# Sample rows added on TensorE and copied by ScalarE, an earlier mark of the prompts' choices, and one expert step ahead of the slot table

## The reference

```python
y  = y + concat(attention, other) @ w_out          # residual, per token
xf = rmsnorm(y, norm_ffn)
g_logits = xf @ router_g + router_g_b              # 4 groups
e_logits = xf @ router_e + router_e_b              # 16 experts
g_idx = argmax(g_logits)                           # one group per token
top_v, top_i = top_k(e_logits in that group, 2)    # two experts per token
y  = y + sum over the two experts of gate * down(silu(gate_e(xf)) * up_e(xf))
```

## Time and profile before

| what | us |
|---|---|
| median of 3 runs | 594.43 |
| the profiled execution | 593.07 |
| its span in the profile | 591.1 |
| TensorE busy in it | 570.3 |
| VectorE, ScalarE, GpSimd busy | 247.6, 154.0, 85.8 |

### The profile page before, as it was taken

How to read it: one execution, slowest core, us unless ns; L and a number is a source line. 1 busy time by engine, 2 the same in 40 slices (tenths; PEclk the granted TensorE clock), 3 DMA queues, 4 the chain that set the end, 5 groups by cost and what they waited for, 6 DMA issues and landing times. The chain is left out here.

```text
span 591.1 us, 8584 instructions
## 1 busy us (share of the span) xinstructions
PE 570.3 (96%) x3462; PEld 322.9 (55%) x3462; DVE 247.6 (42%) x597; ACT 154.0 (26%) x329; POOL 85.8 (15%) x113
## 2 busy tenths in 40 slices
PE   6999999999989999999999999999999999999993
PEld 5677877545733333336977555667655653333331
DVE  6999674213733221145551705251113652221147
ACT  6142185221300101124234203244103310101123
POOL 5991700000012120000100001000000021120000
PEclk9899999999999999999999999999999999999998
DMA  8994899996699999999799998999789999999972
GB/s 333 409 343 63 195 410 368 403 422 277 238 398 406 420 421 420 396 324 414 314 422 330 400 412 299 324 337 409 314 348 416 363 394 411 424 419 419 388 244 92
DMA packets 39930, 208.94 MB, mean 354 GB/s; under 512 B 12819, under 2 KB 14547, under 8 KB 23920
## 3 DMA queue, kind: packets, MB, share of 16 engines
q1 hardware_dynamic: 30416, 169.92, 73.4%
q0 software_dynamic: 7872, 34.53, 16.2%
q10 hardware_dynamic: 1600, 3.90, 1.7%
HBM read 198.76 MB, written 43.74 MB: 410 GB/s over the span
## 5 line engine op out<-in xcount | busy, mean ns | idle before, releaser
L1486 PE MATMUL bank<-arena 128*64 128x512 f32 x264 | 85.4, 598 | 0.0
L1486 PE MATMUL bank<-ring,arena 128*64 128x512 f32 x232 | 74.4, 598 | 0.5 <-DVE arena L1814 0.5
L2273 PE MATMUL bank<-arena,ring 128*128 128x320 f32 x256 | 71.6, 434 | 0.0
L2273 PEld LDWEIGHTS bank<-arena,ring 128*128 128x128 f32 x256 | 48.0, 190 | 21.3 <-issue 1.6
L1410 PE MATMUL bank<-ring,arena 128*128 128x512 f32 x104 | 45.4, 594 | 1.0 <-PEq L451 0.6
L572 PE MATMUL bank<-xnT,ring 128*128 128x320 f32 x144 | 41.2, 447 | 0.5 <-DVE xnT L890 0.5
L1486 PEld LDWEIGHTS bank<-arena 128*64 128x64 f32 x264 | 24.2, 136 | 31.3 <-issue 31.0
L1517 PE MATMUL bank<-arena 128*64 128x512 f32 x136 | 39.8, 594 | 0.7 <-ACT arena L1724 0.7
L1931 DVE COPY arena<-bank 128x512 f32<-128x512 f32 x14 | 9.7, 691 | 68.3 <-PE bank L1517 68.3
L1517 PE MATMUL bank<-ring,arena 128*64 128x512 f32 x120 | 36.1, 593 | 0.7 <-ACT arena L1724 0.7
L1486 PEld LDWEIGHTS bank<-ring,arena 128*64 128x64 f32 x232 | 21.2, 136 | 24.9 <-issue 24.7
(11 more groups left out here) (447 smaller groups left out, 873.0 us busy)
## 6 DMA issues: line engine op xcount, KB each, us to landing
arena<-in_w_moe SPq DMA_DIRECT2D x50, 1024.0 KB, 16.0
ring<-in_w_moe SPq DMA_DIRECT2D x44, 1024.0 KB, 14.3
arena<-in_stream_b SPq DMA_DIRECT2D x4, 2560.0 KB, 14.9
out_o_d_old<-in_cache_d_g POOLq DMA_DIRECT2D x1, 8448.0 KB, 29.9
arena<-in_stream_a SPq DMA_DIRECT2D x4, 2048.0 KB, 11.2
out_o_d_old<-in_cache_d_g POOLq DMA_DIRECT2D x1, 7680.0 KB, 43.6
out_o_d_old<-in_cache_d_g SPq DMA_DIRECT2D x1, 4608.0 KB, 37.8
ring<-in_w_out_even SPq DMA_DIRECT2D x2, 2048.0 KB, 11.9
```

The source lines that it names most:

```text
L1486: last = nc.tensor.matmul(c.bank[2 + j % 2][half, :], xgT[:, j % 2, q, half], w[i][q // 4][:, q % 4, :], start=(q == 0), stop=(q == KC - 1))
L2273: last = nc.tensor.matmul(bank(name)[:, 0:TOK], w[:, k, i * P:(i + 1) * P], xnT[:, k, :], start=(k == 0), stop=(k == KC - 1))
```

## The change

Four edits, in both layers:

1. Samples: TensorE first multiplies the residual rows by the identity into bank 4 and then accumulates `w_out`'s product on top, so PSUM holds the sum. ScalarE copies it to `resid` in two halves and counts up `s_added`; VectorE's `add(2)` is gone.
2. VectorE: `mark(0, 2)` follows `choose(0, 2)` directly, and `place(0, 2)` stands ahead of `mean(2)`.
3. TensorE: the four `keep_clock_up` matmuls ahead of the samples' turn become one, and the one behind `places` is gone.
4. The first step of the first pair's `up` stands ahead of the slot table's product, and VectorE does `first_turned(0)` ahead of `L`.

Beside these, a list of semaphores has two entries instead of three, as many as are used.

```diff
@@ TensorE, samples @@
 def project_samples(first, end):
+    if first == 0:
+        for h in range(2):
+            nc.tensor.matmul(c.bank[4][64 * h:64 * h + 64, :], c.ident[0:64, 0:64],
+                             c.resid[0:64, 2, h * 512:(h + 1) * 512], start=True, stop=False)
     for q in range(first, end):
         for h in range(2):
             last = nc.tensor.matmul(c.bank[4][64 * h:64 * h + 64, :], parts[q][:, SEQ:TOK],
-                                    where[q][:, h * 512:(h + 1) * 512], start=(q == 0), stop=(q == n_parts - 1))
+                                    where[q][:, h * 512:(h + 1) * 512], start=False, stop=(q == n_parts - 1))
@@ TensorE, the list @@
 project_samples(n_parts - 3, n_parts)
-c.keep_clock_up(c.bank[7], 4, 256)
+c.keep_clock_up(c.bank[7], 1, 256)
+pe.wait_ge(s_added, 2)
 turn_rows(2)
 pe.wait_ge(tri_ok, 1)
 pe.wait_ge(sel_ok, 1)
 places((0, 1)).then_inc(pos_pe, 1)
-c.keep_clock_up(c.bank[0], 1, 192)
 logits(2)
...
 gather_first(2)
+up(0, 0, 1)
 pe.wait_ge(H_ok, 1)
 pe.wait_ge(S_ok, 1)
...
-up(0, 0, KC)
+up(0, 1, KC)
@@ ScalarE @@
 for t, rows in enumerate(ROWS):
-    act.wait_ge(added, 2 * t + 2)
+    if t < 2:
+        act.wait_ge(added, 2 * t + 2)
+    else:
+        act.wait_ge(done, 6)
+        for h in range(2):
+            nc.scalar.copy(c.resid[0:rows, 2, h * 512:(h + 1) * 512],
+                           c.bank[4][64 * h:64 * h + 64, :]).then_inc(s_added, 1)
+        act.wait_ge(s_added, 2)
@@ VectorE @@
 choose(0, 2)
-add(2)
 mark(0, 2)
 apply_gain(2)
+place(0, 2)
 mean(2)
-place(0, 2)
 choose(2, 3)
...
+first_turned(0)
 v.tensor_tensor(m["L"], ...).then_inc(S_ok, 1)
-first_turned(0)
 first_turned(1)
```

More of the change, by code:

```diff
@@ L115, in __init__ @@
         self.ring_dn = [nc.alloc_semaphore(f"ring_dn{i}") for i in range(SLOTS)]
-        self.xg_in = [nc.alloc_semaphore(f"xg_in{i}") for i in range(3)]
+        self.xg_in = [nc.alloc_semaphore(f"xg_in{i}") for i in range(XG)]
         self.y_out = [nc.alloc_semaphore(f"y_out{i}") for i in range(2)]
@@ L1179, in moe_block @@
     sel_ok, pos_pe, S0_ok, tmp_ok, idx_pe, idx_ok = s("sel"), s("pe_pos"), s("onehot0"), s("place"), s("pe_idx"), s("idx")
-    lg_read = s("logits_read")
+    lg_read, s_added = s("logits_read"), s("samples_added")
     diag_ok, summed, cnt_ok, g_in, rows_final = s("diag"), s("summed"), s("overflow_count"), s("final_gain"), s("final_out")
@@ L1414, in project_samples @@
             def project_samples(first, end):
+                if first == 0:
+                    for h in range(2):
+                        nc.tensor.matmul(c.bank[4][64 * h:64 * h + 64, :], c.ident[0:64, 0:64], c.resid[0:64, 2, h * 512:(h + 1) * 512],
+                                         start=True, stop=False)
                 for q in range(first, end):
@@ L1418, in project_samples, with turn_rows @@
                         last = nc.tensor.matmul(c.bank[4][64 * h:64 * h + 64, :], parts[q][:, SEQ:TOK],
-                                                where[q][:, h * 512:(h + 1) * 512], start=(q == 0), stop=(q == n_parts - 1))
+                                                where[q][:, h * 512:(h + 1) * 512], start=False, stop=(q == n_parts - 1))
                 if end == n_parts:
                     last.then_inc(done, 2)
-            def turn_rows(t):
+            def turn_rows(t, halves=(0, 1)):
                 rows = ROWS[t]
-                pe.wait_ge(added, 2 * t + 2)
-                for h in range(2):
+                if t < 2:
+                    pe.wait_ge(added, 2 * t + 2)
+                for h in halves:
+                    if t == 2:
+                        pe.wait_ge(s_added, h + 1)
                     for q in range(4):
@@ L1704, in _ @@
             for t, rows in enumerate(ROWS):
-                act.wait_ge(added, 2 * t + 2)
+                if t < 2:
+                    act.wait_ge(added, 2 * t + 2)
+                else:
+                    act.wait_ge(done, 6)
+                    for h in range(2):
+                        nc.scalar.copy(c.resid[0:rows, 2, h * 512:(h + 1) * 512], c.bank[4][64 * h:64 * h + 64, :]).then_inc(s_added, 1)
+                    act.wait_ge(s_added, 2)
                 nc.scalar.activation(xn[0:rows, t], c.resid[0:rows, t], ACT.Square,
@@ L1782, in add @@
                     r = c.resid[0:ROWS[t], t, h * 512:(h + 1) * 512]
-                    ps = c.bank[2 * t + h][0:ROWS[t], :] if t < 2 else c.bank[4][64 * h:64 * h + 64, :]
-                    v.tensor_tensor(r, ps, r, ALU.add).then_inc(added, 1)
+                    v.tensor_tensor(r, c.bank[2 * t + h][:, :], r, ALU.add).then_inc(added, 1)
             def mean(t):
```

## The result

The changed kernel took 598.36 us in the median of 20 runs (594.86 to 606.63), the kernel before 594.41 in the median of 20 (591.45 to 597.17). The ratio is 1.0066, with a 95% interval of 1.0046 to 1.0086: slower by 3.9 us. Both kernels scatter by more than their difference, so that one profile shows one draw. The profiled execution of the changed kernel took 599.21 us.

What follows compares the result with a forecast made beforehand. TensorE, busy 570.3 of 591.1 us, was taken to bound the kernel. 0.05 + 0.05 (both routings) + 2.3 (second gather) = +2.4 us, making the median 596.8; range 594.1 to 599.0.

Steps and rivals of the forecast that it cites:

- a late second gather: Second routing: the gather for the second pair's rows starts 0.7 us late, lands 1.6 slower; TensorE's turn 2.3 us late.
- its own signs: Second routing's profile: granted clock 1.00, gather landing in 5.5 to 8 us; landing in 4.8 makes the forecast wrong.
- a term that stood in the sum as 0: Removing idle matmuls ahead of the samples' turn and logits was counted as costing 0 us.
- The samples' path: Samples' products to their turn: identity products 0.9 us, two copies 1.07 together; the turn begins 0.05 us later per routing.
- its bound: ScalarE's two copies ahead of the samples' turn run one by one, 2 x 0.59 us, making the turn +0.15.
- What is removed was cover, not path: 0.: Ahead of the samples' turn, the removed idle matmuls only filled time when TensorE waited for the add: 0 us.
- Rival C: Clock falls after TensorE's idling around the turns, or loads go first in full: 599 to 605 us, chance 0.10.
- the loads' full price: Second gather waits for the weight loads in full: 0.7 + 3.2 = 3.9 us.
- Place ahead of mean: Second routing: place's move gains nothing, the mean comes 0.6 us later, x_rows is issued about 0.6 us late.
- Up ahead: First up step ahead of the slot table's product: TensorE's sum unchanged, 0; slot table about 0.9 us later, before x_rows lands.
- The gather: Second routing: starts at 478.75, loads at 479.38; lands in 6.4 us, bounds 4.8 and 8.0; turn 2.3 us late.
- the line that the prediction drew through two rows: Gather 1.33 us ahead of the loads landed in 4.8 us, one just behind in 9.3; 3.2 over 1.4 us blamed on loads.

Runs made afterwards that it cites:

- e2: Kernel before with one unread matmul instead of four ahead of the samples' turn and none behind places: 595.47 us, ratio 1.0024.
- e6: Kernel before with all five unread matmuls removed: 598.52 us, ratio 1.0099.
- e3: Kernel before with place(0, 2) moved ahead of mean(2), nothing else: 597.19 us, ratio 1.0030.
- e4: Kernel before with the first up step ahead of the slot table's product and first_turned(0) ahead of L: 593.79 us, ratio 0.9998.
- e5: Changed kernel with unread matmuls fitted to the waits, two of 256 columns and one of 192: 595.87 us, ratio 1.0042.
- e1: Changed kernel with all five unread matmuls back, four of 256 columns and one of 192: 596.76 us, ratio 1.0043.
- e11: The changed kernel run again, unaltered, for a second profile: 596.27 us, ratio 1.0057.
- e12: Changed kernel with fitted unread matmuls (two of 256 columns, one of 192), the same version as e5 run again: 595.36 us, ratio 1.0027.
- e8: Changed kernel with mean ahead of place again, up behind the slot table again, and fitted unread matmuls: 594.72 us, ratio 1.0027.
- e7: Kernel before with two unread matmuls of 256 columns added ahead of a softmax wait in the first mixer: 595.05 us, ratio 1.0036.
- e9: Changed kernel with fitted unread matmuls, second-layer loads of the fourth up step held until the first gather landed: 598.60 us, ratio 1.0086.
- e10: Kernel before with second-layer loads of the fourth up step held until the first gather landed: 596.64 us, ratio 1.0049.

## Why the prediction was right, and where it was wrong

It said 596.8 us, 2.4 more than before, with a range to 599.0. Measured: 3.9 more, 598.36. Direction and size held. Of its mechanism only a part did: of the 2.4 us, 2.3 were to be a late second gather. By its own signs (a gather that lands in 4.8 us, a granted clock other than 1.00) the forecast was wrong in both profiles of the changed kernel: the gather landed in 4.5 and 4.3 us and the clock fell. What was paid there was a term that stood in the sum as 0. That the time still fell into the range is in part luck.

*The samples' path.* Predicted +0.05 us per routing. From the samples' first product to the turn it is now 460.32 to 470.03, 9.71 us, against 9.40 before (from 457.35, where line 1418 begins in its timeline, to 466.75): +0.3. Two terms of the sum were each 0.1 too small: the identity products take 1.0 us and not 0.9, and the copies (580 ns each) do not overlap, 1.18 us and not the 1.07 of the earlier trace rows; the prediction had this last one as its bound.

*"What is removed was cover, not path: 0."* This step failed. The matmuls took no time on the path, but their cover was the clock. e2 and e6 show its price with nothing else changed: 0.24% for four of the five, hardly clear of none, and 1.0% for all. Both profiles of the changed kernel show the fall in the second routing. Rival C had this with a chance of 0.10, together with the loads' full price; against it the prediction set a stretch that idled 1.04 us in 8 without a fall. Such a stretch shows that a fall need not come, not that it will not.

The Trainium skill, "TensorE: Matmul & The Clock Gate", section "Why this matters for your kernels", warns against gaps between bursts of matmuls, but names only longer ones than those that the removed matmuls had filled. By that row alone their removal would have been no risk, other than the prediction read it. The measurement decides: gaps of 0.66 and 0.43 us stood ahead of both falls in the changed kernel.

*Place ahead of mean.* `x_rows` 0.6 us later: measured 0.55 (470.03 to 473.54, against 2.96). Right. Its landing was taken as 0.7 late; in the profile of e3 the gather was not late at all (11.31 us behind the turn, 11.30 before).

*Up ahead.* Predicted 0, measured +0.2 per layer (e4's profile), within the noise of its times. The slot table was to come 0.9 us later and before `x_rows` landed: its product came 1.1 us later in e4 (the sum had taken 2/3 of the first gather for its third quarter), and in the profile of the changed kernel, where the clock's fall came on top, the gather waited for the table.

*The gather.* Predicted: issued 0.63 us ahead of the loads, 6.4 us to landing, 2.3 us lost, as one fixed number. The profiles of the second routing, by the time between gather and loads: 0.26 us, 9.1 to landing (e2); 0.86, 6.8 (e5); 1.0, 4.7 (e1); 1.2, 4.3 (e11); 1.3, 4.7 to 5.1 (before, e3, e12); 1.4, 5.7 (e8); 1.5 to 1.8, 4.5 to 5.1 (e4, e6, changed, e7). The direction of the line that the prediction drew through two rows is borne out, on two late gathers, one of them in an execution that was the longest of its kernel. Its slope is not: 3.2 us over 1.4 would give 7.2 and 5.9 us for these two. And e8's 5.7 us, like e9's 5.4 with the loads held back, shows that the time to landing also moves without the loads.

What the prediction took for fixed is a draw: with no fall of the clock at the place, the gather began 10.8 us behind the samples' turn in e7 and 12.4 in e2, in both of which `x_rows` was issued 2.96 us behind it. In both profiles of the changed kernel the fallen clock delayed the fourth up step and so these loads, and the gather got away: the two losses may exclude one another, as far as two profiles tell.

The Trainium skill's rule of round-robin between queue rows ("DMA: Bandwidth & Descriptors", section "Queues, rings and completion order") would let the gather's 512 KB go at half the rate. With 1.3 us for them at the full rate, as in the prediction, that is an estimate of 1.3 us more than the 4.8. The 6.8 and 9.1 us are more than that.

What the pieces are worth together, as far as the runs tell them apart: instructions, 0.5 us per routing (0.3 at the turn, 0.2 at up), 1.0; beside them the clock's fall (3.2 and 1.6 us in the two profiles of the changed kernel) or TensorE's wait for the gather (0.4, 2.6 and 0.4 in e1, e5 and e12). Restoring the matmuls in full or fitted gives 1.0043, 1.0042 and 1.0027, against 1.0066 and 1.0057 as changed: the intervals overlap, so the times alone don't show the clock's share. The granted clock of every execution, which is on record beside its time, says more:

| executions | number | mean clock |
|---|---|---|
| kernel before, beside e1 to e12 | 111 | 0.9922 |
| changed kernel (the 20 of the result, e11) | 32 | 0.9872 |
| changed, matmuls back or fitted (e1, e5, e12) | 36 | 0.9917 |
| e2, four of five removed | 13 | 0.9896 |
| e6, all removed | 10 | 0.9827 |
| e3, no matmul touched | 12 | 0.9894 |

An estimate: a mean clock lower by 0.001 costs 0.6 us of the 595, as TensorE is nearly always busy. So e6's 0.0100 against its own rounds (0.9927) is 5.9 us, about its whole loss. e3 lies 0.003 low without a matmul touched, so that a difference of this size, e2's for one, proves little alone. The changed kernel lies 0.0045 below its versions with the matmuls back (95% interval 0.0023 to 0.0066, over different chips), an estimated 2.7 us; its mean time is only 1.3 us longer, 597.90 against 596.58. With the matmuls back the clock is that of the kernel before, and the mean time is still 2.7 us longer than its 593.89. 1.0 of these are the instructions above (2.2 in e1, with its 0.6 per layer); the rest is the wait for the gather and what the runs don't tell apart. Nothing tried beats the kernel before; e4 equals it.

## What to carry to other kernels

An unread matmul that ends before a wait does costs nothing and may be what keeps the clock; take its length from the wait, and judge its removal by many executions, by their times and their granted clocks, not by the chain of one. When a step is moved by half a microsecond, look at what is issued just behind it on another queue: a gather that had 1.3 us on a pair of 1 MB loads landed in 4.8 us, one with 0.3 us in 9.1. And hold one profile against the scatter of the runs before reading a cause from it.

## What the runs showed that was not expected

The kernel's time scatters by 1% from execution to execution, and the profiles show four places that make it: the 48 instructions of line 582, about 6 us or 8; a fall of the clock to 0.50 between 14 and 22 us (before, changed, e1, e3, e7, e8 and e12, not the others); another between 96 and 108 us (e1, e2, e3 and e9); and the last stretch from the second pair's turn to the end, 108 us or 110 (e7, e9, e10, and e2 with a fallen clock; 109.4 in e5 with a fallen clock). None of them is touched by the change, and each is worth 1.7 us or more (for the falls an estimate, half of the 3.4 us that the shortest lasted), about as much as the effect that was sought. What draws them stays open.
